# Hybrid trunk layer on one core: the last activation sums spread over four down units, the first down chunk merged, and a later wait in the opening matmuls

## The chip, the cores and the metric

One core of a Trainium2 chip runs the whole layer in float32 precision. The metric is the device time in microseconds (us) of one launch. Engines: TensorE (PE, its weight loads PEld), VectorE (DVE), ScalarE (ACT), GpSimd (POOL) and SyncE (SP), which issues most DMAs; ACT issues the others. `SPq` and `ACTq` in a row are the DMA-issuing instructions of SP and ACT.

## The reference, cut to what matters

```
h  = RMSNorm(x);  p = h @ W_in
y  = concat[SSD(p), sparse attention(p), short conv(p)] @ W_out
x2 = x + y;  h2 = RMSNorm(x2)
g  = causal_conv3(h2 @ W_gate)
out = x2 + (silu(g) * (h2 @ W_up)) @ W_down       # 512 tokens, D = 2048, D_FF = 5632
```

## The kernel before

Every float32 operand is split into a high and a low part in fp32r (`hi = round(x)`, `lo = x - hi`), and a product is three matmuls: hi*hi, lo*hi, hi*lo. ACT makes the high part of a weight block, POOL (for two of seven blocks DVE) the low part.

*The opening.* `quarter` (line 673) multiplies four 128x128 blocks of one projection tile: per block k it issues whi*hhi (L681), wlo*hhi (L682) and whi*hlo (L683). The activations h arrive meanwhile: ACT makes `hhi[k]` (L1137, semaphore `h_hi`), DVE then `hlo[k]` (L1608, `h_lo`). In the first eight quarters those with even n wait for `h_lo` of k ahead of all three matmuls; the odd ones use the same k again. Each quarter first waits for its `wlo` (L599, `lo_ready`).

*The MLP* runs in 44 gate/up units and then 40 down units, called FT, FT+1, ..., FT+39. A unit is one 2x2 block product done with seven products instead of eight (sums of weight blocks times sums of activation blocks). Its positions 0 to 6 each take κ blocks of 128 (κ = 8 in gate/up, 4 or 5 in down). The seven weight operands come from four loaded blocks A21, A22, A11, A12: A21 is copied to PSUM by ACT (`copy_a21`, L1215), DVE forms the sums from it (`sum1`, `sum2`, `sum3_`, `sum4_`), ACT writes `fhi` (`high_unit`, L1208), POOL or DVE `flo` (`low_unit` L629, `low_s1`, `low_s2`), PE multiplies (`product`). All engines run their instructions in the order of the program. While PE is in unit u, ACT does in this order: high 2, high 3, high 4, **copy_a21 of unit u+1**, high 5, high 6, high 0 and high 1 of u+1. POOL does low 3, 4, 5, 6 and low 0 of u+1. SP does, for a unit u, A21 (once `sum3_` of u-1 is done), A22, A11, A12 (once POOL has done low 3 of u-1), and then what hangs behind the unit: `load_x2` and one `load_chunk`.

*Down* goes over five chunks of eight units (one unit per pair of output tiles), κ = 4, 4, 5, 4, 5. Chunk c multiplies by the activation pairs `PAIRS[c]`, brought from HBM by `load_chunk`, seven positions each with a high and a low transfer of 384 KB. The chunk 0 transfers are issued by ACT: positions 0 to 4 in unit FT-1, position 5 behind high 2 and position 6 behind high 3 of unit FT. Those of chunk 1 are issued by SP, one position behind each of the units FT+1 to FT+7. A **merged** unit (`merged(u)`, L869 and L870) joins hi*hi and hi*lo into one matmul 512 wide, since the high and low activations lie side by side; DVE then adds two halves per product (L1840 and L1842) where an unmerged unit (L876 to L878, three matmuls 256 wide) needs one addition (L1842). Before the change all gate/up units and chunks 1 to 4 are merged; chunk 0 (units FT to FT+7) is not, and its fourth block lies in `thi`, `tlo`.

*Where down begins.* The last gate tile is still unfinished in unit FT: ACT's `first_tap` (L1231), two taps on DVE (L1735), ACT's silu (L1291), DVE's `activate` (L1745), and then `act_sums` (L1753, L1754, L1757, L1760), four sums of activation blocks that make the seven operands of the last pair. ACT (L1269, L1270) and POOL (L647, L648) split them in unit FT+1; POOL's last step raises `t_lo` to FP = 22. The residual tiles come back by `load_x2(p)`, for unit FT+p. Four of them (p = 4 to 7) go to places that the activations use until then, so SP waits ahead of them:

```
if u == FT + 3:  sp_.wait_ge(t_lo, FP);  load_x2(4); load_x2(5)
if u == FT + 4:  sp_.wait_ge(f_act, FT); load_x2(6); load_x2(7)
```

Of the kernel before, what the change touches and what calls it, by code (L numbers as in the profile page):

```python
# [169 lines left out]
def hybrid_block(nc, xT, w_in, w_out, w_gu, w_dn, params, relb, cmats, onehot, bias_rows, acs_rows, x2_rows, act_hi, act_lo, out):  # L170
# [4 lines left out]
    with ExitStack() as ctx:  # L175
# [59 lines left out]
        thi = at(RING + 26 * KB, "thi", [P, 7, HT], F32R)  # L235
        tlo = at(RING + 33 * KB, "tlo", [P, 7, HT], F32R)
# [5 lines left out]
        fifth = at(RING + 26 * KB, "fifth", [P, 7, 2, HT], F32R)  # L242
# [213 lines left out]
        def x2_tile(d):  # L456
            return (x2a[:, d, :] if d < 2 else x2b[:, d - 2, :] if d < 6 else x2c[:, d - 6, :] if d < 8 else x2b[:, d - 4, :] if d < 12
                    else x2d[:, d - 12, :] if d < 14 else upv[:, :] if d == 14 else sqsum[:, :])

        def pieces(c, b):  # L460

            half, pairs = 4 * (c % 2), PAIRS[c]
            run = [m for m in pairs[:4] if m < FP - 2]
            found = [(block_of(b)[:, part, half:half + len(run), :], store[b, :, run[0]:run[0] + len(run), :])
                     for part, store in ((HI, act_hi), (LO, act_lo))]
            if len(pairs) == 5:
                found += [(fifth[:, b, part, :], store[b, :, pairs[4], :]) for part, store in ((HI, act_hi), (LO, act_lo))]
            return found
# [126 lines left out]
        def _(pool):  # L595
# [76 lines left out]
        def _(pe):  # L672
            def quarter(slot, n, dst, src_hi, src_lo, ks, first, last, before=None):

                pe.wait_ge(lo_ready, n + 1)
# [182 lines left out]
            def product(u, pos, dst, fresh, before=None):  # L858
# [3 lines left out]
                for k in range(n):  # L862
# [116 lines left out]
        def _(sc):  # L979
# [257 lines left out]
            def unit(n):  # L1237
# [114 lines left out]
        def _(ve):  # L1352
# [495 lines left out]
            def down_unit(n):  # L1848
# [185 lines left out]
```

## Time and profile before

| | us |
|---|---|
| three runs | 2112.37, 2112.72, 2119.51; median 2112.72 |
| the profiled execution | 2116.9 |
| its span, first to last instruction | 2115.1 |
| PE busy in the span | 2104.3 (99%) |
| DVE, POOL, ACT busy | 1555.0, 1276.4, 1008.6 |

The profiled execution is 1.8 us longer than its span. Matmuls are pipelined and their ends are modelled, so progress of PE is read from starts and from its idle times. Engines other than PE have idle time nearly everywhere; the question at each place is whose result PE takes last.

### The profile page before, as it was taken

The numbers are of one execution on the slowest core, as the hardware profiler recorded it, in microseconds if no ns is written. First come the engines' busy times: TensorE is split into PE (matmuls) and PEld (weight loads), VectorE is DVE, ScalarE is ACT, GpSimd is POOL, SyncE is SP. The second block draws the span as 40 slices with busy tenths as digits, with TensorE's granted clock in tenths as the row PEclk, the third lists the DMA queues.
The fourth block names the chain that finished last, engine by engine and source line by source line (L and its number), as shares of the span: only waits on it lengthen the run. The fifth ranks groups of instructions, "written<-read, shape, count | busy, mean of one in ns | idle before, by whom it ended". The sixth has DMA issues, their size and how long they took to land.

```text
span 2115.1 us, 34610 instructions
## 1 busy us (share of the span) xinstructions
PE 2104.3 (99%) x11476; PEld 1782.6 (84%) x11476; DVE 1555.0 (74%) x2756; ACT 1008.6 (48%) x1468; POOL 1276.4 (60%) x731
## 2 busy tenths in 40 slices
PE   9999999999999999999999999999999999999999
PEld 6777777887888888888888888888888899888888
DVE  6489565457663226888888888888888768988987
ACT  6343344434433446545545555555555544444443
POOL 5345334444545656667767767767767676666665
PEclk9999999999999999999999999999999999999999
DMA  6224123233333443344544544544544766655743
GB/s 210 84 74 126 63 69 100 95 105 102 103 99 125 146 145 134 136 164 140 169 154 145 171 144 144 169 152 141 166 151 148 260 222 209 212 187 189 234 130 125
DMA packets 150119, 308.76 MB, mean 146 GB/s; under 512 B 13272, under 2 KB 54424, under 8 KB 149880
## 3 DMA queue, kind: packets, MB, share of 16 engines
q1 hardware_dynamic: 103568, 250.39, 35.3%
q10 hardware_dynamic: 46440, 56.94, 8.6%
q8 instruction: 63, 1.03, 0.2%
q14 instruction: 48, 0.39, 0.1%
HBM read 261.64 MB, written 45.51 MB: 145 GB/s over the span
## 4 chain that ended last, share of the span: by engine, by line
PE 92%; DVE 6%; issue 1%; ACT 0%; DMA 0%; ACTq 0%; SPq 0%; DVEq 0%
PE ps L870 38%; PE ps L869 20%; PE ps L681 10%; PE ps L683 9%; PE ps L682 9%; PE ps L876 1%; PE ps L878 1%; PE ps L877 1%; DVE work L1458 1%; DVE work L1457 1%; DVE work L1361 1%; PE ps L777 1%; DVE work L1360 1%; PE ps L763 0%; PE ps L749 0%
## 5 line engine op out<-in xcount | busy, mean ns | idle before, releaser
L870 PE MATMUL ps<-comb,fhi 128*128 128x512 f32 x3360 | 1180.5, 394 | 0.0
L869 PE MATMUL ps<-comb,flo 128*128 128x256 f32 x3360 | 943.6, 281 | 0.0
L870 PEld LDWEIGHTS ps<-comb,fhi 128*128 128x128 f32 x3360 | 629.8, 187 | 143.9
L629 POOL TENSOR_TENSOR flo<-raw,fhi 128x1024 fp32r<-128x1024 f32 (+2 forms) x252 | 485.0, 1934 | 361.8 <-ACT fhi L1208 361.0
L869 PEld LDWEIGHTS ps<-comb,flo 128*128 128x128 f32 x3360 | 634.4, 189 | 5.6 <-DVE ps L1817 2.2
L599 POOL TENSOR_TENSOR wlo<-raw,whi 128x512 fp32r<-128x512 f32 x260 | 361.4, 1403 | 394.9 <-ACT whi L988 344.1
L629 POOL TENSOR_TENSOR flo<-sum,fhi 128x1024 fp32r<-128x1024 f32 (+2 forms) x168 | 324.0, 1936 | 41.0 <-ACT fhi L1208 40.5
L1208 ACT ACTIVATE fhi<-ps 128x1024 fp32r<-128x1024 f32 (+2 forms) x168 | 141.7, 844 | 420.1 <-DVE ps L1699 242.5
L681 PE MATMUL ps<-hhi,whi 128*128 128x512 f32 x784 | 317.3, 405 | 2.4 <-DVE hlo L1608 2.4
L683 PE MATMUL ps<-hlo,whi 128*128 128x512 f32 x784 | 306.4, 391 | 0.0
L682 PE MATMUL ps<-hhi,wlo 128*128 128x512 f32 x784 | 305.7, 390 | 0.0
L1208 ACT ACTIVATE fhi<-raw 128x1024 fp32r<-128x1024 f32 (+2 forms) x252 | 219.4, 871 | 45.7 <-PE ps L870 36.2
L681 PEld LDWEIGHTS ps<-hhi,whi 128*128 128x128 f32 x784 | 147.2, 188 | 49.3 <-issue 13.9
L683 PEld LDWEIGHTS ps<-hlo,whi 128*128 128x128 f32 x784 | 147.1, 188 | 31.8
L682 PEld LDWEIGHTS ps<-hhi,wlo 128*128 128x128 f32 x784 | 147.4, 188 | 30.5 <-issue 2.2
L1208 ACT ACTIVATE fhi<-sum 128x1024 fp32r<-128x1024 f32 (+2 forms) x168 | 146.1, 870 | 16.1 <-PE ps L870 11.2
L988 ACT ACTIVATE whi<-raw 128x512 fp32r<-128x512 f32 x200 | 118.5, 621 | 61.0 <-PE ps L683 33.0
L682 PE MATMUL ps<-yhi,wlo 128*128 128x512 f32 x256 | 99.6, 389 | 0.0
L683 PE MATMUL ps<-ylo,whi 128*128 128x512 f32 x256 | 99.6, 389 | 0.0
L681 PE MATMUL ps<-yhi,whi 128*128 128x512 f32 x256 | 99.6, 389 | 0.0
L1215 ACT ACTIVATE ps<-raw 128x1024 f32<-128x1024 f32 (+2 forms) x84 | 70.6, 841 | 35.7 <-DVE sum L1716 32.0
L1675 DVE TENSOR_TENSOR ps<-ps,raw 128x1024 f32<-128x1024 f32 (+2 forms) x84 | 83.5, 995 | 4.9 <-DMA raw<-w_gu 4.0
(246 smaller groups left out, 2799.2 us busy)
## 6 DMA issues: line engine op xcount, KB each, us to landing
raw<-w_gu SPq DMA_DIRECT2D x176, 512.0 KB, 3.4
raw<-w_in SPq DMA_DIRECT2D x196, 256.0 KB, 3.2
raw<-w_dn SPq DMA_DIRECT2D x96, 256.0 KB, 2.9
raw<-w_dn SPq DMA_DIRECT2D x64, 320.0 KB, 3.1
act_hi<-thi ACTq DMA_DIRECT2D x20, 896.0 KB, 4.2
act_lo<-tlo ACTq DMA_DIRECT2D x20, 896.0 KB, 8.2
raw<-w_out SPq DMA_DIRECT2D x64, 256.0 KB, 3.2
comb<-act_hi SPq DMA_DIRECT2D x21, 512.0 KB, 3.9
```

Of the source, the lines that this page charges most:

```text
L599: nc.gpsimd.tensor_tensor(wlo[:, slot % NW, 0:width], raw[:, slot % NRAW, 0:width], whi[:, slot % NW, 0:width].bitcast(F32), ALU.subtract) ...
L629: nc.gpsimd.tensor_tensor(flo[s][:, 0:w], src[:, 0:w], fhi[s][:, 0:w].bitcast(F32), ALU.subtract).then_inc(f_lo_pool, 1)
L681: nc.tensor.matmul(dst, whi[:, s, w], src_hi[:, k, :], start=first and i == 0, stop=False)
L682: nc.tensor.matmul(dst, wlo[:, s, w], src_hi[:, k, :], start=False, stop=False)
L683: ins = nc.tensor.matmul(dst, whi[:, s, w], src_lo[:, k, :], start=False, stop=last and i == len(ks) - 1)
L777: nc.tensor.matmul(ps[:, 2 + hh, 0:P * (b + 1)], qkT[rows, h // 2, b * P:(b + 1) * P], qkT[rows, 4 + h // 2, 0:P * (b + 1)], start=True, s ...
L869: nc.tensor.matmul(dst[:, 0:HT], flo[s][:, w], both[:, HI, :], start=fresh and k == 0, stop=False, skip_group_check=True)
L870: ins = nc.tensor.matmul(dst, fhi[s][:, w], both, start=False, stop=k == n - 1, skip_group_check=True)
L988: A(whi[:, slot % NW, 0:width], raw[:, slot % NRAW, 0:width], ACT.Copy).then_inc(hi_ready, 1)
L1208: A(fhi[s][:, 0:w], src[:, 0:w], ACT.Copy).then_inc(f_hi, 1)
L1215: A(wide(LEFT)[:, 0:width(u)], raw21[:, 0:width(u)], ACT.Copy).then_inc(copied21, 1)
L1675: V.tensor_tensor(wide(RIGHT)[:, 0:w], wide(LEFT)[:, 0:w], raw22[lane(u) % 2][:, 0:w], ALU.add).then_inc(sum1_ready, 1)
```

## The change

1. Opening: a quarter with even n waits for `h_hi` ahead of the first two matmuls of a block and for `h_lo` only ahead of the third.
2. Unit FT keeps three matmuls; FT+1 to FT+7 become merged. `thi` and `tlo` become the halves of one tile `pair_sums`, which is also what chunks 2 and 4 used as `fifth`.
3. ACT in unit FT: the transfers of position 5 are issued behind `first_tap`, those of position 6 behind high 4.
4. The four last sums on DVE leave unit FT: one in each of FT+1 and FT+2, two in FT+3. ACT's and POOL's split of them moves from unit FT+1 to FT+4.
5. SP: behind unit FT+3 it waits for `f_act` and loads x2 for p = 4 and 5 (now to `x2d`, `upv`, `sqsum`); behind unit FT+5 it waits for `t_lo` = FP and loads p = 6 and 7 (now to `x2b`).

```diff
         def merged(u):
-            return gate_up(u) or u >= FT + NPAIR
+            return gate_up(u) or u > FT
+        def apart(u, k):
+            return not gate_up(u) and k == (3 if u < FT + NPAIR else 4)
...
-                if u == FT + 3:
-                    sp_.wait_ge(t_lo, FP)
+                if u == FT + 3:
+                    sp_.wait_ge(f_act, FT)
                     load_x2(4)
                     load_x2(5)
-                if u == FT + 4:
-                    sp_.wait_ge(f_act, FT)
+                if u == FT + 5:
+                    sp_.wait_ge(t_lo, FP)
                     load_x2(6)
                     load_x2(7)
...
# POOL, behind low 0 of the next unit (ACT the same, behind high 4)
-                if lane(n) % 2 == 1 and n != 1 and (gate_up(n) or n == FT + 1):
+                if lane(n) % 2 == 1 and n != 1 and gate_up(n) or n == FT + 4:
...
# quarter()
                     nc.tensor.matmul(dst, wlo[:, s, w], src_hi[:, k, :], start=False, stop=False)
+                    if between is not None:
+                        between(k)
                     ins = nc.tensor.matmul(dst, whi[:, s, w], src_lo[:, k, :], start=False,
...
-                        (lambda k: pe.wait_ge(h_lo, k + 1)) if n % 2 == 0 else None)
+                        (lambda k: pe.wait_ge(h_hi, k + 1)) if n % 2 == 0 else None,
+                        (lambda k: pe.wait_ge(h_lo, k + 1)) if n % 2 == 0 else None)
...
# ACT, unit FT
-                if n == FT:
-                    load_chunk(sc, 0, 5)
                 sc.wait_ge(loaded12, lin(n, 16, 16))
                 high_unit(n, 3, raw12)
-                if n == FT:
-                    load_chunk(sc, 0, 6)
...
                     first_tap(step(n, -1))
+                if n == FT:
+                    load_chunk(sc, 0, 5)
                 sc.wait_ge(sum3_ready, lin(n, 1, 1))
                 high_unit(n, 4, sum3)
+                if n == FT:
+                    load_chunk(sc, 0, 6)
...
# DVE, down_unit
+            def last_sum(i):
+                buf = act[(FP - 1) % 2]
+                to, a, b = ((2, 0, 1), (4, 6, 0), (3, 6, 2), (5, 7, 3))[i]
+                ve.wait_ge(f_act, FT)
+                ve.wait_ge(t_sum, 4 * (FP - 1) + (0, 0, 1, 3)[i])
+                V.tensor_tensor(buf[:, to, :], buf[:, a, :], buf[:, b, :], ALU.subtract).then_inc(t_sum, 1)
...
+                if 1 <= v <= 3:
+                    last_sum(v - 1)
                 accumulate(v, 3, 0, early, xbank(n))
...
-                if tail:
-                    act_sums(n, 2)
+                if v == 3:
+                    last_sum(3)
```

## Rows read from the trace of the kernel before

**Rows 1.** The page: busy times of the engines; shares of the chain that ended last.
```profile
PE 2104.3 (99%) x11476; PEld 1782.6 (84%) x11476; DVE 1555.0 (74%) x2756; ACT 1008.6 (48%) x1468; POOL 1276.4 (60%) x731
...
PE 92%; DVE 6%; issue 1%; ACT 0%; DMA 0%; ACTq 0%; SPq 0%; DVEq 0%
```

**Rows 2.** Waits of PE, whole span: total us, times, longest.
```profile
PE ps L681 <- DVE hlo L1608: 2.4, 2, 1.6
...
PE ps L876 <- DVE x2a L1842: 1.5, 1, 1.5
```

**Rows 3.** Timeline of the opening: start, us, engine, line, operation, [idle before].
```profile
5.80 1.27 POOL L599 TENSOR_TENSOR wlo<-raw,whi 128x512 fp32r<-128x512 f32 x1 [5.34 <-ACT whi L988]
...
7.76 0.47 PE L681 MATMUL ps<-hhi,whi 128*128 128x512 f32 x1 [1.64 <-DVE hlo L1608]
...
9.31 1.41 DVE L1608 SCALAR_TENSOR_TENSOR hlo<-resid,pc,hhi 128x512 fp32r<-128x512 f32 x2 [1.03 <-ACT hhi L1137]
...
10.12 0.50 PE L681 MATMUL ps<-hhi,whi 128*128 128x512 f32 x1 [0.73 <-DVE hlo L1608]
...
10.69 0.40 PE L683 MATMUL ps<-hlo,whi 128*128 128x512 f32 x1
```

**Rows 4.** PE timeline: first matmuls of units FT+1, FT+4, FT+8, FT+15.
```profile
1685.86 0.28 PE L876 MATMUL ps<-comb,fhi 128*128 128x256 f32 x1
...
1716.22 0.28 PE L876 MATMUL ps<-comb,fhi 128*128 128x256 f32 x1
...
1756.54 0.28 PE L869 MATMUL ps<-comb,flo 128*128 128x256 f32 x1
...
1825.35 0.28 PE L869 MATMUL ps<-comb,flo 128*128 128x256 f32 x1
```

**Rows 5.** Timelines of ACT, DVE and PEld in unit FT.
```profile
1674.11 2.28 ACTq L480 DMA_DIRECT2D comb<-act_hi  x1
1676.41 0.46 ACTq L480 DMA_DIRECT2D comb<-act_lo  x1
1676.99 0.69 ACT L1231 ACTIVATE ps<-gpad,pc 128x512 f32<-128x512 f32 x1 [2.33 <-issue]
...
1682.39 1.49 DVE L1754 TENSOR_TENSOR act<-act 128x256 f32<-128x256 f32 x1
...
1684.32 0.19 PEld L876 LDWEIGHTS ps<-comb,fhi 128*128 128x128 f32 x1 [1.65 <-DMA comb<-act_lo]
```

**Rows 6.** DMA issues between 1676.41 and 1676.7: KB, us to landing.
```profile
comb<-act_lo ACTq DMA_DIRECT2D x1, 384.0 KB, 7.5
```

**Rows 7.** The page, DMA issues of the whole span: one group.
```profile
raw<-w_dn SPq DMA_DIRECT2D x96, 256.0 KB, 2.9
```

**Rows 8.** DVE timeline: one act_sums, and DVE's idle in merged unit FT+10.
```profile
1685.99 0.41 DVE L1760 TENSOR_TENSOR act<-act 128x256 f32<-128x256 f32 x1
...
1780.64 0.42 DVE L1840 TENSOR_TENSOR x2b<-ps,x2b 128x256 f32<-128x256 f32 x1 [0.49 <-PE ps L870]
```

**Rows 9.** POOL timeline, end of unit FT+1.
```profile
1698.22 0.74 POOL L648 TENSOR_TENSOR comb<-act,comb 128x256 fp32r<-128x256 f32 x1
```

**Rows 10.** SP timeline, behind A12 of unit FT+3, then behind A12 of FT+5.
```profile
1700.63 0.94 SPq L531 DMA_DIRECT2D x2b<-x_rows  x2
1701.68 0.40 SPq L480 DMA_DIRECT2D comb<-act_hi  x1
...
1703.19 6.08 SPq L522 DMA_DIRECT2D raw<-w_dn  x4
...
1719.46 0.37 SPq L480 DMA_DIRECT2D comb<-act_hi  x1
...
1723.34 6.09 SPq L522 DMA_DIRECT2D raw<-w_dn  x4
```

**Rows 11.** ACT and POOL: copy of A21 to low 5, in unit FT+3.
```profile
1709.80 0.60 ACT L1215 ACTIVATE ps<-raw 128x512 f32<-128x512 f32 x1 [1.33 <-DMA raw<-w_dn]
...
1711.03 1.29 POOL L629 TENSOR_TENSOR flo<-sum,fhi 128x512 fp32r<-128x512 f32 x1 [1.13 <-ACT fhi L1208]
```

More of the change, by code:

```diff
@@ L234, in hybrid_block @@
         act = [at(RING + 10 * KB + 8 * KB * i, f"act{i}", [P, 8, HT]) for i in range(2)]
-        thi = at(RING + 26 * KB, "thi", [P, 7, HT], F32R)
-        tlo = at(RING + 33 * KB, "tlo", [P, 7, HT], F32R)
+        pair_sums = at(RING + 26 * KB, "pair_sums", [P, 7, 2, HT], F32R)
+        thi, tlo = pair_sums[:, :, 0, :], pair_sums[:, :, 1, :]
         x2b = at(RING + 10 * KB, "x2b", [P, 8, T])
@@ L239, in hybrid_block @@
         x2d = at(yq(6, 1), "x2d", [P, 2, T])
-        fifth = at(RING + 26 * KB, "fifth", [P, 7, 2, HT], F32R)
         ctx.enter_context(nc.sbuf_tensor("reserved", [P, (EXTRA + 16 * KB) // 4], F32))
@@ L456, in x2_tile @@
         def x2_tile(d):
-            return (x2a[:, d, :] if d < 2 else x2b[:, d - 2, :] if d < 6 else x2c[:, d - 6, :] if d < 8 else x2b[:, d - 4, :] if d < 12
-                    else x2d[:, d - 12, :] if d < 14 else upv[:, :] if d == 14 else sqsum[:, :])
+            return (x2a[:, d, :] if d < 2 else x2b[:, d - 2, :] if d < 6 else x2c[:, d - 6, :] if d < 8 else x2d[:, d - 8, :] if d < 10
+                    else upv[:, :] if d == 10 else sqsum[:, :] if d == 11 else x2b[:, d - 8, :])
         def pieces(c, b):
@@ L466, in pieces @@
             if len(pairs) == 5:
-                found += [(fifth[:, b, part, :], store[b, :, pairs[4], :]) for part, store in ((HI, act_hi), (LO, act_lo))]
+                found += [(pair_sums[:, b, part, :], store[b, :, pairs[4], :]) for part, store in ((HI, act_hi), (LO, act_lo))]
             return found
@@ L524, in load_x2 @@
             def load_x2(p):
-                if p == NPAIR - 1:
+                if p == 5:
                     sp_.dma_start(upv[:, :], x2_rows[2 * p]).then_inc(x2_loaded[p], 16)
@@ L529, in load_x2 @@
                     return
-                dst = {1: x2b[:, 0:2, :], 2: x2b[:, 2:4, :], 3: x2c[:, :, :], 4: x2b[:, 4:6, :], 5: x2b[:, 6:8, :], 6: x2d[:, :, :]}[p]
+                dst = {1: x2b[:, 0:2, :], 2: x2b[:, 2:4, :], 3: x2c[:, :, :], 4: x2d[:, :, :], 6: x2b[:, 4:6, :], 7: x2b[:, 6:8, :]}[p]
                 sp_.dma_start(dst, x2_rows[2 * p:2 * p + 2].rearrange("d p t -> p d t")).then_inc(x2_loaded[p], 16)
@@ L639, in unit @@
                     low_unit(step(n, 1), 0, raw11)
-                if lane(n) % 2 == 1 and n != 1 and (gate_up(n) or n == FT + 1):
-                    m = lin(n, 1, -3) // 2 if isinstance(n, int) else 2 * n[0] + (n[1] - 3) // 2
+                if lane(n) % 2 == 1 and n != 1 and gate_up(n) or n == FT + 4:
+                    m = FP - 1 if n == FT + 4 else (n - 3) // 2 if isinstance(n, int) else 2 * n[0] + (n[1] - 3) // 2
                     pool.wait_ge(t_hi, m + 1)
-                    if n == FT + 1:
+                    if n == FT + 4:
                         last = act[(FP - 1) % 2]
@@ L672, in _, with quarter @@
         def _(pe):
-            def quarter(slot, n, dst, src_hi, src_lo, ks, first, last, before=None):
+            def quarter(slot, n, dst, src_hi, src_lo, ks, first, last, before=None, between=None):
                 pe.wait_ge(lo_ready, n + 1)
@@ L866, in product @@
                     if merged(u):
-                        both = fifth[:, b] if k == 4 and not gate_up(u) else block_of(b)[:, :, half + k, :]
+                        both = pair_sums[:, b] if apart(u, k) else block_of(b)[:, :, half + k, :]
                         nc.tensor.matmul(dst[:, 0:HT], flo[s][:, w], both[:, HI, :], start=fresh and k == 0, stop=False, skip_group_check=True)
@@ L871, in product @@
                         continue
-                    if u < FT + NPAIR and k == 3:
+                    if apart(u, k):
                         high, low = thi[:, b, :], tlo[:, b, :]
@@ L1262, in unit @@
                     load_chunk(sc, 0, 0)
-                if lane(n) % 2 == 1 and n != 1 and (gate_up(n) or n == FT + 1):
-                    m = pair_of(n)
+                if n == FT:
+                    load_chunk(sc, 0, 6)
+                if lane(n) % 2 == 1 and n != 1 and gate_up(n) or n == FT + 4:
+                    m = FP - 1 if n == FT + 4 else pair_of(n)
                     sc.wait_ge(t_sum, 4 * m + 4)
-                    if n == FT + 1:
+                    if n == FT + 4:
                         last = act[(FP - 1) % 2]
@@ L1858, in down_unit @@
                 if v < NPAIR:
-                    ve.wait_ge(x2_loaded[v], 16 if v < NPAIR - 1 else 32)
+                    ve.wait_ge(x2_loaded[v], 32 if v == 5 else 16)
                 accumulate(v, 1, 0, late, xbank(n))
@@ L1877, in down_unit @@
                     sum3_(n + 1)
-                if tail:
-                    act_sums(n, 0)
                 ve.wait_ge(d_add, 7 * v + 2)
```

3 lines of the change are left out of this document (removed).

## The prediction

> **What bounds the kernel now.** I read the page first: PE is busy 2104.3 of 2115.1 us, and the chain that ended last is PE for 92% and DVE for 6% [rows 1]. So whatever is gained must be idle time of PE or spacing between its matmuls, and whatever makes another engine late counts only when PE has to wait for it. The list of PE's waits comes next: of its few entries two lie at the places of this change, 2.4 us in two waits for `hlo` (the opening) and one of 1.5 us for DVE in unit FT [rows 2]. Last come the timelines at both places, for what arrives last there, and SP's timeline around the moved loads.
>
> PE's pace: from FT+4 to FT+8 four unmerged units take 1756.54 - 1716.22 = 40.32 us, 10.08 each, with no gap; from FT+8 to FT+15 seven merged ones take 68.81 us, 9.83 each [rows 4].
>
> **Step 1, the opening.** The first real matmul starts at 7.76, released by hlo[0]; but `wlo` of the quarter, for which PE waits in any case, is ready only at 5.80 + 1.27 = 7.07 [rows 3]. The high parts come earlier. So the first block starts near 7.2, and its third matmul, which still needs hlo[0], near 7.73 instead of two matmuls after 7.76: about 0.55 earlier. That lead dies at block 2, where PE waits again: hlo[2] releases it at 10.12, and the third matmul is at 10.69 [rows 3]. DVE started hlo[2] at 9.31, as soon as ACT had hhi[2], so the two high matmuls can run between 9.4 and 10.0 and the third goes at about 10.12 to 10.15. The gain that remains is 10.69 - 10.13 = 0.55 us. After that block PE waits for `hlo` no more (two waits in all [rows 2]), and everything there is made from the loads and not from PE's progress. Later, around 90 to 200 us, DVE is on the chain; it is fed by PE's results there, so I let the lead pass, with 0 as the other bound. **-0.55.**
>
> **Step 2, unit FT.** The wait named for PE is DVE's, which did two of the sums ahead of an addition that PE's position 6 wanted; the second of them alone holds DVE from 1682.39 for 1.49 us. The sums go, and `first_tap` no longer stands behind a transfer whose issue held ACT for 2.28 us: `first_tap` ran at 1676.99 after 2.33 us of idle ACT [rows 5]. With both gone the addition ends some 2 us earlier, about 1682.2, in time for PE, which was ready at 1684.32 - 1.65 = 1682.67. But the weight load that PE resumed with, at 1684.32, is put down to something else, the transfer of `act_lo` [rows 5], issued at 1676.41 and landed 7.5 us later, at 1683.9 [rows 6]. That is the new last arrival. And the change issues it later: position 5 behind `first_tap` (1675.3 and 1675.7), position 6 behind high 4, which waits for DVE's `sum3` (1676.7) and takes 0.6, so at about 1677.4 and 1677.8, 1.4 later than before. At 7.5 us it would land at 1685.3, and PE would resume 1.1 us later than now. A 256 KB piece lands in 2.9 us in the median of the span [rows 7]; at that pace, 1680.7, it would cost nothing, a gain of 1.65 and with a short wait for low 4 ahead of it 2.1. The transfers of position 5 are out of the way later too, and the same bytes have to pass, so I take the middle: PE resumes where it does now. **0, between -2.1 and +1.1.** If the 2.28 us hold of ACT comes again it stands ahead of high 4 instead of `first_tap`, and then costs up to the same 1.1.
>
> The Trainium skill ("DMA: Bandwidth & Descriptors", section "Queues, rings and completion order") says that each DMA engine takes turns between the queues that have work for it. Here SP puts 512 KB pieces into its queue from 1677 on, so by that rule ACT's late pieces would get half the engines; a landing of 7.5 us for 384 KB agrees with a shared stretch. By that rule step 2 would be nearer its upper end, +1.1.
>
> **Step 3, merged units.** 10.08 - 9.83 = 0.25 us less per unit [rows 4]. Not the third matmul's cost: the columns are the same, 768 per block, only the start intervals are shorter. Five units get it freely (FT+1 to FT+3, FT+6, FT+7), FT+4 and FT+5 are counted in step 5. DVE pays 7 more additions per unit, and had 0.49 idle in the one gap of a merged unit [rows 8]; so it is close to being the bound but not it, as seven units of chunk 1 show. 5 x 0.25: **-1.2.** Bounds: 0 (DVE eats it) and -1.4.
>
> **Step 4, the last sums.** Each is 0.41 us of DVE, some 0.35 when pipelined [rows 8]. In FT+1 and FT+2 one fits into the 0.49. FT+3 has two: 0.7 to 0.8 against 0.49. **+0.2**, between 0 and +0.9.
>
> **Step 5, SP waits for the split of the last sums.** This is the term that decides. SP issues in order. Behind A12 of FT+5 it will wait for `t_lo` = FP and only then issue load_x2(6), load_x2(7), one `load_chunk`, and after these **A21, A22, A11 and A12 of unit FT+6**. Take S4 = start of unit FT+4 on PE, S5 and S6 the next ones.
> - When SP is there: A12(FT+5) is issued once POOL has done low 3 of FT+4; what is behind it stands at 1719.46 with S4 = 1716.22, S4 + 3.2. The next A21 is at 1723.34, S4 + 7.1 [rows 4, 10].
> - When `t_lo` comes: the split has moved from POOL's unit FT+1 to its unit FT+4, behind low 0 of the next unit. In FT+1 it ended at 1698.22 + 0.74 = 1698.96 with that unit's start at 1685.86: start + 13.1 [rows 4, 9]. So S4 + 13.1, and SP sits for 9.9 us. Before, the waiting unit was two units behind the splitting one (FT+3 and FT+1): SP passed at 1700.63, 1.7 after `t_lo`, and the wait cost nothing [rows 9, 10].
> - A21(FT+6) is then issued at about S4 + 15.0 (two x2 issues, two of the chunk, 0.4 to 0.5 each). It was copied by ACT at S5 + 2.4 = S4 + 12.2 in the ordinary run of things (the copy of FT+4's A21, which waited 1.33, ran at 1709.80, so ACT was ready for it at 1708.5, in unit FT+3, which started 10.08 ahead of 1716.22, at 1706.14) [rows 4, 11]. So it is late however fast it lands.
> - When it lands: the same sequence (two x2 pieces, one chunk position, A21) stood behind FT+3. From the first issue at 1700.63 to the copy that waited for A21, 1709.80, are 9.2 us [rows 10, 11]. In the new place the queue is empty before it, so 8.8: S4 + 13.2 + 8.8 = S4 + 22.0.
> - What is queued behind: ACT stands at copy_a21(FT+6) and with it high 5 and 6 of FT+5 and high 0 and 1 of FT+6; DVE stands at sum1(FT+6). Copy to low 5 on POOL is 1711.03 - 1709.80 = 1.23, low 5 takes 1.29, and 0.1 to PE [rows 11]: PE's position 5 of FT+5 starts at S4 + 24.65. It would want S4 + 9.83 + 5 x 1.40 = 16.85. Two positions later, S6 = S4 + 27.45. Low 6 and low 0 follow POOL's low 5 at 1.29 each, in time; DVE catches up in the same stretch.
> - Also in it: POOL's low 3 of FT+5 comes behind the split, at S4 + 14.4, where PE wants it at 14.0; 0.4 us that vanish in the larger stall.
>
> Before, S6 - S4 was 20.16. **+7.3.** Bounds: A21 landing in 2.9 us [rows 7] gives S6 = S4 + 17.9 + 2.65 + 2.8 = 23.35, so +3.2; the full 9.2 and a ragged restart, +8.
>
> **Sum**, against the profiled execution: -0.55 + 0 - 1.2 + 0.2 + 7.3 = +5.75, so 2116.9 + 5.75 = 2122.7 (span 2115.1 + 5.75, and 1.8 around it). That execution was 4.2 above the median of the runs, 2112.72, and the difference is not in the trace's parts that change; on the median it is **2118.5 us**. The other steps (other places for x2 tiles, `pair_sums` for `fifth`) move the same bytes at the same rate: nothing.
>
> **Rivals.**
> - *The hold of SP costs nothing* (it ends faster). It would need A21(FT+6) landed by S4 + 12.2, so `t_lo` by S4 + 3.4; below that point each us is a us of PE. For it speaks only that the trace before had the same wait for free, against it the program order on POOL. Price: FT+4 and FT+5 merged, 2 x 0.25 less and 0.4 for low 3, so -1.65 in all, and -3.7 if unit FT loses its stall too: 2109.0 to 2111.1, say 2110.5. 12%.
> - *The hold costs, but the queue empties fast.* A21 lands between S4 + 17.9 [rows 7] and S4 + 20, halfway to the forecast's 22.0: total +1.6 to +3.7, 2114.3 to 2116.4. For it: nothing else is in flight in that hold. Against: 9.2 us in rows 10 and 11, with little else in flight either. 23%.
> - *The transfers of positions 5 and 6 come too late as well*, and DVE falls behind in FT+3: +1.1 and +0.9 on top, 2119.5 to 2122. 13%.
> - That the opening doesn't gain, since `wlo` comes last, is inside the forecast: 7.07 bounds it.
>
> The Trainium skill ("DMA: Bandwidth & Descriptors", section "Anatomy of one DMA") prices a transfer at 2.0 us fixed and its bytes at 436 GB/s (a fit for another issue path). An estimate by it for the 2.0 MB up to and with A21: 6.8 us instead of 8.8, the landing at S4 + 20.0, 2116.5; the 2.9 us of a quiet 256 KB piece agrees with it (2.6), the 9.2 of the full sequence does not.
>
> **How the numbers follow.** Forecast 52%, rivals 12, 23 and 13%. The forecast's own range is 2116.5 to 2120.5. The range of 8 in 10 reaches over the fast-queue case and most of the last: 2113.0 to 2122.5, also since one of three runs before was 6.8 above the others. What a measurement can tell from no change is some 0.5%, 10.6 us: faster than 2102.2 is in no case (1%), slower than 2123.3 needs the worst ends together (4%), within it 95%. The sign is slower with 0.86.
>
> **What would show it.** In the changed trace: PE's first matmul near 7.2 and the first wait for `hlo` at a third matmul; in unit FT PE resumes position 6 released by DMA, not by DVE; merged units FT+1 and FT+2 take 9.8; SP idle for some 10 us behind A12 of FT+5, released by POOL, and in unit FT+5 one PE idle time of about 7.8 us ahead of position 5, with ACT waiting for `raw<-w_dn` at L1215. If there is no PE gap above 1 us in FT+5 or FT+6, the forecast is wrong and the kernel should be faster; if the gap is 3 to 5 us, only the landing was mis-sized.

## The result: the changed kernel is slower by 0.2 to 0.4%

| | before | after |
|---|---|---|
| median of 9 runs each | 2112.72 | 2121.63 (2119.87 to 2125.9), ratio 1.0039 [1.0027, 1.0051] |
| a second comparison, 35 and 12 runs | 2113.67 | 2118.65 (2115.24 to 2125.26), ratio 1.0021 [1.0007, 1.0035] |
| profiled execution / its span | 2116.9 / 2115.1 | 2121.12 / 2119.2 |

The forecast, 2118.5, is a ratio of 1.0027. By the prediction's bound of 0.5% this is no change in either comparison, but both intervals exclude 1. The medians differ by 8.9 and by 5.0 us, for a forecast of 5.8, and two terms were off; both have to be explained. The three comparisons below ran on three chips (medians of the kernel before: 2111.18, 2113.67 and 2117.06), so a median is set beside its own comparison only.

Lines have moved by 3 to 6 in the changed kernel: L681 and L683 are L684 and L688; L869 and L870 are L875 and L876; L876 to L878 are L882 to L884; `high_unit` is L1214, `copy_a21` L1221, `low_unit` L632.

The page after, busy times (for [rows 1]):
```profile
PE 2103.6 (99%) x11280; PEld 1776.3 (84%) x11280; DVE 1570.8 (74%) x2805; ACT 1008.4 (48%) x1468; POOL 1275.6 (60%) x731
...
PE 91%; DVE 6%; DMA 1%; issue 1%; ACT 1%; POOL 0%; SPq 0%; ACTq 0%; DVEq 0%
```
PE has 196 matmuls less (7 units x 28 blocks, merged), DVE 49 additions more (7 x 7), and DMA has come into the chain. The waits of PE after, total, times, longest (for [rows 2]):
```profile
PE ps L875 <- POOL flo L632: 6.2, 1, 6.2
PE ps L837 <- DVE work L1596: 1.5, 1, 1.5
PE ps L809 <- DVE work L1552: 0.9, 1, 0.9
PE ps L684 <- POOL wlo L602: 0.9, 1, 0.9
PE ps L684 <- ACT hhi L1143: 0.7, 1, 0.7
PE ps L882 <- DMA comb<-act_lo: 0.6, 1, 0.6
```
The waits for `hlo` and for DVE in unit FT are gone from this list. Three short ones stand in their places (`wlo`, `hhi`, `act_lo`), and there is one new wait, by far the longest: 6.2 us for low 5. It is in unit FT+5. Starts on PE of units FT, FT+4, FT+6 and FT+8 after (for [rows 4]):
```profile
1673.35 0.28 PE L882 MATMUL ps<-comb,fhi 128*128 128x256 f32 x1
...
1713.81 0.28 PE L875 MATMUL ps<-comb,flo 128*128 128x256 f32 x1
...
1742.59 0.28 PE L875 MATMUL ps<-comb,flo 128*128 128x256 f32 x1
...
1762.29 0.28 PE L875 MATMUL ps<-comb,flo 128*128 128x256 f32 x1
```
FT to FT+8 is 88.94 us, against 82.93 before (1673.61 to 1756.54). So the profiled pair's +4.1 of span is -0.26 up to unit FT, +6.01 in these eight units, and -1.6 in the remaining 357 us, which the change leaves as they were but for the places of tiles (that last figure is no effect of the change; see the last section).

The timeline after, around the hold: SP's issues, then who was released by them.
```profile
1711.42 6.27 SPq L525 DMA_DIRECT2D raw<-w_dn  x4
1726.89 0.89 SPq L534 DMA_DIRECT2D x2b<-x_rows  x2
1727.89 0.40 SPq L483 DMA_DIRECT2D comb<-act_hi  x1
1728.33 0.43 SPq L483 DMA_DIRECT2D comb<-act_lo  x1
1728.86 2.37 SPq L525 DMA_DIRECT2D raw<-w_dn  x4
...
1734.86 0.60 ACT L1221 ACTIVATE ps<-raw 128x512 f32<-128x512 f32 x1 [8.63 <-DMA raw<-w_dn]
1735.56 0.70 DVE L1681 TENSOR_TENSOR ps<-ps,raw 128x512 f32<-128x512 f32 x1 [6.30 <-DMA raw<-w_dn]
1736.08 1.27 POOL L632 TENSOR_TENSOR flo<-sum,fhi 128x512 fp32r<-128x512 f32 x1 [6.72 <-ACT fhi L1214]
...
1737.41 0.58 PE L875 MATMUL ps<-comb,flo 128*128 128x256 f32 x1 [6.16 <-POOL flo L632]
...
1738.22 0.42 PE L875 MATMUL ps<-comb,flo 128*128 128x256 f32 x1
...
1738.86 0.42 PE L875 MATMUL ps<-comb,flo 128*128 128x256 f32 x1
```
Read it downwards. SP has issued the weights of FT+5 and then issues nothing for 9.2 us (1711.42 + 6.27 = 1717.69 to 1726.89): it stands at the wait for `t_lo`. Then it first issues two x2 tiles and two chunk transfers, and only at 1728.86 the A21 of unit FT+6. ACT, DVE and POOL have been idle for 6 to 9 us when it lands, and all of them and PE resume within 2.6 us. So what looks like a stall of every engine at once, with the DMA engines full, is here one late load. The last two rows show something more: blocks follow at 1738.86 - 1738.22 = 0.64 us, where a merged block otherwise takes 0.35.

Stretches of 5 us after (us, busy of PE, PEld, DVE, ACT, POOL, granted clock, DMA share, GB/s):
```profile
1730.00:1735.00 5.00, 1.25 (x7) 0.80 (x5) 0.00 (x0) 0.14 (x1) 0.00 (x0) 1.00 1.04 391
1735.00:1740.00 5.00, 2.59 (x8) 2.31 (x9) 3.40 (x7) 2.52 (x5) 3.75 (x3) 0.56 0.84 300
1740.00:1745.00 5.00, 5.00 (x23) 4.29 (x23) 3.59 (x8) 1.86 (x3) 1.30 (x1) 0.76 0.30 96
```
After 6.16 us of idle time PE is granted 0.56 and then 0.76 of its clock, so for part of both stretches the lower of its two levels, 1.2 instead of 2.4 GHz. Positions 5 and 6 take 2.73 and 2.45 us instead of 1.4 each.

### The profile page after: what moved, and what is told of

Read it like the earlier page. It is cut to its first block, busy times and chain, and to the rows that moved or that the text cites. A ratio compares the mean times of both kernels' runs of the same rounds, so it can differ in the third digit from the quotient of the medians.

```text
span 2119.2 us, 34271 instructions
## 1 busy us (share of the span) xinstructions
PE 2103.6 (99%) x11280; PEld 1776.3 (84%) x11280; DVE 1570.8 (74%) x2805; ACT 1008.4 (48%) x1468; POOL 1275.6 (60%) x731
## 4 chain that ended last, share of the span: by engine, by line
PE 91%; DVE 6%; DMA 1%; issue 1%; ACT 1%; POOL 0%; SPq 0%; ACTq 0%; DVEq 0%
PE ps L876 40%; PE ps L875 20%; PE ps L684 10%; PE ps L688 9%; PE ps L685 9%; DVE work L1464 1%; DVE work L1463 1%; DVE work L1367 1%; DVE work L1366 1%; PE ps L782 1%; PE ps L768 0%; PE ps L754 0%; DVE work L1455 0%; DVE work L1442 0%; PE ps L823 0%
## 5 line engine op out<-in xcount | busy, mean ns | idle before, releaser
L876 PE MATMUL ps<-comb,fhi 128*128 128x512 f32 x3507 | 1234.5, 395 | 0.0
L875 PE MATMUL ps<-comb,flo 128*128 128x256 f32 x3507 | 987.7, 282 | 6.2 <-POOL flo L632 6.2
L876 PEld LDWEIGHTS ps<-comb,fhi 128*128 128x128 f32 x3507 | 659.6, 188 | 146.7
L632 POOL TENSOR_TENSOR flo<-raw,fhi 128x1024 fp32r<-128x1024 f32 (+2 forms) x252 | 484.7, 1934 | 360.9 <-ACT fhi L1214 360.5
L875 PEld LDWEIGHTS ps<-comb,flo 128*128 128x128 f32 x3507 | 664.1, 189 | 12.8 <-POOL flo L632 6.6
L632 POOL TENSOR_TENSOR flo<-sum,fhi 128x1024 fp32r<-128x1024 f32 (+2 forms) x168 | 323.9, 1934 | 46.8 <-ACT fhi L1214 46.6
L1214 ACT ACTIVATE fhi<-ps 128x1024 fp32r<-128x1024 f32 (+2 forms) x168 | 141.7, 843 | 421.4 <-DVE ps L1705 255.9
L684 PE MATMUL ps<-hhi,whi 128*128 128x512 f32 x784 | 317.7, 405 | 1.5 <-POOL wlo L602 0.9
L688 PE MATMUL ps<-hlo,whi 128*128 128x512 f32 x784 | 307.0, 392 | 0.1
L1214 ACT ACTIVATE fhi<-raw 128x1024 fp32r<-128x1024 f32 (+2 forms) x252 | 219.4, 871 | 41.2 <-PE ps L876 39.2
L684 PEld LDWEIGHTS ps<-hhi,whi 128*128 128x128 f32 x784 | 147.4, 188 | 47.8 <-issue 13.9
L688 PEld LDWEIGHTS ps<-hlo,whi 128*128 128x128 f32 x784 | 147.2, 188 | 32.8 <-DVE hlo L1614 0.9
L1214 ACT ACTIVATE fhi<-sum 128x1024 fp32r<-128x1024 f32 (+2 forms) x168 | 146.1, 870 | 14.2 <-PE ps L876 12.4
L684 PE MATMUL ps<-yhi,whi 128*128 128x512 f32 x256 | 99.7, 390 | 0.0
L688 PE MATMUL ps<-ylo,whi 128*128 128x512 f32 x256 | 99.7, 389 | 0.0
L1221 ACT ACTIVATE ps<-raw 128x1024 f32<-128x1024 f32 (+2 forms) x84 | 70.6, 841 | 47.1 <-DVE sum L1722 34.0
L1681 DVE TENSOR_TENSOR ps<-ps,raw 128x1024 f32<-128x1024 f32 (+2 forms) x84 | 83.5, 994 | 10.3 <-DMA raw<-w_dn 6.3
```

What stands on the lines that cost most here:

```text
L632: nc.gpsimd.tensor_tensor(flo[s][:, 0:w], src[:, 0:w], fhi[s][:, 0:w].bitcast(F32), ALU.subtract).then_inc(f_lo_pool, 1)
L684: nc.tensor.matmul(dst, whi[:, s, w], src_hi[:, k, :], start=first and i == 0, stop=False)
L875: nc.tensor.matmul(dst[:, 0:HT], flo[s][:, w], both[:, HI, :], start=fresh and k == 0, stop=False, skip_group_check=True)
L876: ins = nc.tensor.matmul(dst, fhi[s][:, w], both, start=False, stop=k == n - 1, skip_group_check=True)
L1214: A(fhi[s][:, 0:w], src[:, 0:w], ACT.Copy).then_inc(f_hi, 1)
L1221: A(wide(LEFT)[:, 0:width(u)], raw21[:, 0:width(u)], ACT.Copy).then_inc(copied21, 1)
```

## The experiments

All stand on the changed kernel unless it is said. "Stretch" is FT to FT+8 by PE's starts in the profiled execution: 82.93 before, 88.94 after.

**1. `sp_later`: the wait and what it guards one unit later.**
```diff
-                if u == FT + 5:
+                if u == FT + 6:
                     sp_.wait_ge(t_lo, FP)
                     load_x2(6)
                     load_x2(7)
```


> The changed kernel with one edit: the wait for t_lo = FP and load_x2(6), load_x2(7) stand behind unit FT+6 on SP instead of FT+5. Theory (the hold of SP in FT+5 is the whole loss): PE's idle of 6.2 us ahead of position 5 of FT+5 and the stretch at the lower clock behind it go; from the start of FT+4 to that of FT+6 take 20.0 to 20.2 us instead of 28.8 (two merged units of 9.83 and 0.4 for POOL's low 3, which still comes behind the split). The kernel then ends some 3 us below the one before the change: 2109 to 2111, ratio 0.998 to 0.9995. Rival (the merged units or the later transfers cost, the hold only hides it): a new PE wait of over 1 us appears in FT+3 to FT+7 and the time stays above 2113.

Measured: 2109.49 (2107.61 to 2113.4, 11 runs) beside 2111.18 (33 runs), ratio 0.9991 [0.9982, 1.0000]; stretch 80.35. FT+4 starts at 1716.88, POOL's split ends at 1729.99, and SP is at the wait only after that (timeline of `sp_later`, POOL and SP):
```profile
1729.24 0.75 POOL L651 TENSOR_TENSOR comb<-act,comb 128x256 fp32r<-128x256 f32 x1
```
```profile
1725.13 6.47 SPq L525 DMA_DIRECT2D raw<-w_dn  x3
1731.65 0.94 SPq L534 DMA_DIRECT2D x2b<-x_rows  x2
```
```profile
1736.98 0.28 PE L875 MATMUL ps<-comb,flo 128*128 128x256 f32 x1
```
The wait costs nothing where it now stands, 1.66 us behind the split, as the same wait did before the change. FT+4 and FT+5 take 1736.98 - 1716.88 = 20.10 us instead of 28.78. The whole loss was in the place of one wait and of the two loads behind it; experiment 3 parts them. The 20.10 lies in the expected range for a reason only partly right: of the 0.44 us above two units of 9.83, some 0.3 is not low 3 but a late addition of DVE, told under steps 3 and 4.

**2. `warm`: PE kept busy in the gap** by 24 extra matmuls into an unused bank, ahead of position 5 of FT+5 (they add no result).
```diff
+                    if v == 5 and pos == 5:
+                        for _ in range(24):
+                            nc.tensor.matmul(bank(X), comb[:, 0, HI, 0, 0:P], block_of(0)[:, :, 0, :], ...)
```


> The changed kernel with 24 matmuls more, 512 wide, on PE ahead of its wait for position 5 of unit FT+5; they read activations that lie in SBUF and write a PSUM bank that nobody uses at that time, 24 x 0.23 = 5.5 us of the 6.2 us idle. Theory (the lower clock behind the idle costs by itself): the granted clock stays 1.00 from 1735 to 1745, positions 5 and 6 of FT+5 take 1.4 us each instead of 2.73 and 2.45, the unit is 2.2 to 2.5 us shorter (16.3 instead of 18.64), and the time is 2 to 2.5 us under that of the changed kernel. Rival (the slow positions are the refill of ACT, POOL and DVE behind the hold): the unit stays 18.5 or so whatever the clock.

Measured: 2116.21 (2114.42 to 2125.71, 11 runs) beside the same 2111.18, ratio 1.0024 [1.0015, 1.0034]. PE in `warm`, and its stretches (columns as above):
```profile
1736.24 5.65 PE L942 MATMUL ps<-comb 128*128 128x512 f32 x24
1742.71 0.39 PE L875 MATMUL ps<-comb,flo 128*128 128x256 f32 x1 [0.82 <-POOL flo L632]
```
```profile
1735.00:1740.00 5.00, 5.00 (x25) 4.13 (x25) 0.00 (x0) 0.00 (x0) 0.00 (x0) 1.00 1.04 403
1740.00:1745.00 5.00, 4.18 (x22) 3.25 (x21) 3.86 (x9) 2.67 (x5) 3.62 (x3) 1.00 0.80 297
```
The load is as late as before (DMA at 403 GB/s, three engines idle), but the clock stays at 1.00, and from position 5 to S6 it takes 2.93 us instead of 5.18 (after) and 4.40 (after, second trace). So the lowered clock costs 1.5 to 2.3 us here, and the wait itself the rest. This is read from the traces; the ratio of `warm` lies between the two ratios of the changed kernel (1.0039 and 1.0021), so the runs alone don't show it. The Trainium skill ("TensorE: Matmul & The Clock Gate", section "What's actually happening") has the rule: "the default state is throttled, and activity releases the throttle". The traces agree with it (0.56 behind the gap, 1.00 with the gap filled), and with it the forecast could have had this term.

**3. `hold_only`: the wait stays behind FT+5, the two x2 loads go behind FT+6.**
```diff
                 if u == FT + 5:
                     sp_.wait_ge(t_lo, FP)
+                if u == FT + 6:
                     load_x2(6)
                     load_x2(7)
```


> The changed kernel with load_x2(6) and load_x2(7) behind unit FT+6, but the wait for t_lo = FP kept behind FT+5. It tells the hold from the 1 MB in the queue ahead of A21(FT+6). Theory (both count, the hold first): A21 is issued 0.9 us earlier and has 0.77 MB less... 1.0 MB less ahead of it; ACT copies it at start of FT+4 + 18 to 19 instead of + 21.05, PE idles 3 to 4 us instead of 6.2, and the time is 2.5 to 4 us under that of the changed kernel. If the hold alone mattered (landing 3 us behind an issue): + 17, idle 2 us. If the bytes alone mattered: no idle of PE above 1 us.

Measured: 2114.82 (2112.37 to 2116.19, 10 runs), ratio 1.0014 [1.0004, 1.0023]; stretch 88.02. ACT and PE in `hold_only`:
```profile
1730.21 0.60 ACT L1222 ACTIVATE ps<-raw 128x512 f32<-128x512 f32 x1 [6.79 <-DMA raw<-w_dn]
```
```profile
1732.76 0.58 PE L876 MATMUL ps<-comb,flo 128*128 128x256 f32 x1 [4.40 <-POOL flo L633]
```
FT+4 starts at 1710.96, so A21 lands by S4 + 19.25 (after: 21.05). 1 MB of x2 ahead of it costs 1.8 us; the wait alone still leaves PE idle for 4.4 us, and the clock is lowered all the same (0.70 and 0.62 in the two stretches from 1730), so that S6 - S4 is 27.1. The wait for `t_lo` alone makes 7.0 of the 8.7 us between `sp_later` and the changed kernel, the loads in front of A21 the rest. The landing and the idle time are a little above what was expected (18 to 19 and 3 to 4); the expectation had no term for the clock. The loads without the wait were not tried.

**4. `opening_only`: the kernel before, with step 1 alone.**
```diff
+                        (lambda k: pe.wait_ge(h_hi, k + 1)) if n % 2 == 0 else None,
                         (lambda k: pe.wait_ge(h_lo, k + 1)) if n % 2 == 0 else None)   # ahead of the third matmul
```


> The kernel before with the opening part of the change alone. Theory: PE's third matmul of block 2 starts near 10.15 instead of 10.69, 0.54 us earlier, and the lead is kept to the end: time 0.5 us under that of before, which a measurement can't tell from none (ratio 0.998 to 1.002). Rival: the lead is lost again where DVE is on the chain, 90 to 200 us, so that PE's start behind it differs by under 0.2 us.

Measured: 2110.73 (2108.95 to 2113.72, 10 runs) beside 2111.18, ratio 1.0000 [0.9990, 1.0009]. In its profile PE is 0.44 us ahead up to 155 us and 0.29 from 203 us on, where PE waits for DVE's `work` (L1391) 0.5 us against 0.4 before; gate/up starts at 811.00 against 811.29. Some 0.15 of the lead is given back at that wait. 0.29 us is below what the runs can tell.

**5. `after_again`: the changed kernel, unaltered,** in one comparison with the next three.

> The changed kernel once more, unaltered, to be compared on the chip and in the rounds of the next three. Its trace showed 5.0 to 5.5 us more than the kernel before in the stretches that the change touches, its runs 8.9 us. Theory (the rest is the spread of runs): the ratio comes out nearer 1.0025 than 1.004, and the stretch from the start of unit FT to that of FT+8 takes 88.9 us again. Rival (something outside the stretch costs 3 to 4 us in every run): ratio 1.004 or more again.

Measured: the second row of the first table; stretch 88.23, FT 11.12, FT+4 and FT+5 28.0. The stretch is the same to 0.7 us; most of the 3 us between the two medians of the changed kernel is not in it.

**6. `unmerged`: `sp_later` with FT+1 to FT+7 in three matmuls again.**
```diff
-            return gate_up(u) or u > FT
+            return gate_up(u) or u >= FT + NPAIR
```


> The kernel sp_later with chunk 0 unmerged as before the change. Theory (a merged unit saves 0.25 us): FT+1 to FT+7 take 10.08 each but for FT+5 with about 10.2, the stretch from FT to FT+8 takes 1.7 us more than in sp_later (80.35), 82.0; time +1.7 us, below what 3 rounds tell apart. Rival (DVE's seven further additions eat the saving): the stretch is within 0.5 us of sp_later's.

Measured: 2115.15 (10 runs) beside 2113.67, ratio 0.9994 [0.9980, 1.0009]; units 10.08 us each again (FT+5 10.19), stretch 81.76 against 80.35. Merging is worth 1.4 us over seven units, 0.20 each, where [rows 4] gave 0.25.

**7. `old_order`: `sp_later` with ACT's transfers of positions 5 and 6 at their places before the change** (behind high 2 and high 3, ahead of `first_tap`). The last sums stay spread.
```diff
                     high_unit(n, 2, wide(LEFT))
+                if n == FT:
+                    load_chunk(sc, 0, 5)
                 sc.wait_ge(loaded12, lin(n, 16, 16))
                 high_unit(n, 3, raw12)
...
+                if n == FT:
+                    load_chunk(sc, 0, 6)
...
                     first_tap(step(n, -1))
-                if n == FT:
-                    load_chunk(sc, 0, 5)
                 sc.wait_ge(sum3_ready, lin(n, 1, 1))
                 high_unit(n, 4, sum3)
...
-                if n == FT:
-                    load_chunk(sc, 0, 6)
```


> The kernel sp_later with the transfers of positions 5 and 6 issued by ACT where they were before the change, behind high 2 and high 3 of unit FT. It tells what shortened FT from 12.25 to 10.96 us. Theory (first_tap ahead of the transfers does it, since the additions and low 4 follow from it): FT is 11.8 to 12.3 us long, with a wait of 0.4 or more ahead of position 4 and one ahead of position 6, released by DMA, of 1.3 to 1.6. Rival (the sums' leaving DVE does it): FT stays at 11.0 to 11.2, with no wait ahead of position 4.

Measured: 2113.0 (12 runs), ratio 0.9989 [0.9974, 1.0004]; stretch 81.92, FT 12.60 (before 12.25, after 10.96). ACT in `old_order`, then the weight load of position 6:
```profile
1671.64 2.49 ACTq L483 DMA_DIRECT2D comb<-act_lo  x1
1674.26 0.69 ACT L1237 ACTIVATE ps<-gpad,pc 128x512 f32<-128x512 f32 x1 [2.43 <-issue]
```
```profile
1681.84 0.19 PEld L882 LDWEIGHTS ps<-comb,fhi 128*128 128x128 f32 x1 [1.82 <-DMA comb<-act_lo]
```
Without the sums DVE is not late, and unit FT is as long as it was: position 4 waits 0.35 us for low 4, and the weights of position 6 wait 1.82 us for the transfer. One trace each would not be enough here, since unit FT differs from one execution to the next, but the twelve traces together bear it out, with one overlap. With ACT's old order it took 12.25, 11.82 and 12.90 us with the sums in it (`before`, `before_again`, `opening_only`) and 12.60 without; with the new order it took 10.96 to 11.64 in seven kernels or traces, and 12.19 in `x2_later`. So ACT's order, not the sums, shortened unit FT, by about 1.1 us.

**8. `x2_later`: `sp_later` with `load_x2(2)` and `load_x2(3)` behind FT+2 instead of FT+1,** to take SP's bytes out of the way of ACT's last transfer.
```diff
-                if u == FT + 1:
+                if u == FT + 2:
                     load_x2(2)
                     sp_.wait_ge(up_part, 2 * FT)
                     load_x2(3)
```


> The kernel sp_later with load_x2(2) and load_x2(3), 1 MB, behind unit FT+2 instead of FT+1 on SP. In unit FT PE waits 0.8 to 1.3 us ahead of position 6 for the last act_lo transfer of position 6, which lands 6.7 us behind its issue. Theory (SP's transfers share the DMA engines with it): it lands within 4.5 to 5.5 us, the wait is under 0.3 us, FT takes 10.1 to 10.4 us instead of 11.1, and the time is 0.8 us under that of sp_later. Rival (the order in ACT's own queue sets the landing): FT stays at 11.0 or more.

Measured: 2113.36 (12 runs), ratio 0.9989 [0.9979, 0.9999]; FT 12.19, not the 10.1 to 10.4 expected. It was no cleaner: the two chunk 1 transfers behind them moved up in their place, and an issue held ACT for 1.84 us, so that the last `act_lo` was issued at S(FT) + 3.21 and landed 7.4 us later. Inconclusive, hence the next.

**9. `quiet_sp`: `sp_later` with nothing but weights and the first x2 piece from SP until behind FT+2.**
```diff
-                if u == FT + 1:
+                if u == FT + 2:
                     load_x2(2)
+                    load_chunk(sp_, 1, 0)
+                if u == FT + 3:
                     sp_.wait_ge(up_part, 2 * FT)
                     load_x2(3)
...
                     load_x2(4)
+                if u == FT + 4:
                     load_x2(5)
```


> The kernel sp_later with nothing of SP's in the DMA queues, but weights and the first x2 piece, while ACT's transfers of positions 5 and 6 land: load_x2(2) and position 0 of chunk 1 stand behind unit FT+2, load_x2(3) and (4) behind FT+3, load_x2(5) behind FT+4. In x2_later the 1 MB of x2 alone was moved and its place in the queue was taken at once by chunk 1's 768 KB. Theory (it is the share of the engines, whoever takes it): the last act_lo lands 4.5 to 5.5 us behind its issue instead of 6.7 to 7.4, the wait ahead of position 6 is under 0.3 us, FT takes 10.1 to 10.5 us; time 0.7 us under sp_later's, which is below what the rounds tell apart. Rival (ACT's four pieces set their own landing): FT stays at 11.0 or more.

Measured: 2115.26 (12 runs) beside 2117.06 (17), ratio 0.9992 [0.9978, 1.0005]; stretch 80.60, FT 11.05. The last `act_lo` lands 6.5 us after its issue (after: 6.7), and position 6 still waits:
```profile
1686.78 0.19 PEld L882 LDWEIGHTS ps<-comb,fhi 128*128 128x128 f32 x1 [0.93 <-DMA comb<-act_lo]
```
The bulk that SP issues behind FT+1 is not what makes it late; what is left is ACT's own 384 KB pieces, the weights and the first x2 piece. Which of these sets the 6.5 us stays open.

**10. `before_again`: the kernel before, one more profiled execution,** for the scatter of its trace.

> The kernel before, unaltered, for a second trace: how much its stretches differ from one execution to the next. Theory: the stretch from the start of FT to that of FT+8 is 82.9 to 83.7 us again and gate/up starts at 811.3; what differs beyond 1 us lies in the pace of the matmuls, 0.347 or 0.353 us per merged pair, over long stretches. Rival: the stretch itself moves by over 1 us.

Measured: 2112.4, span 2110.6; stretch 82.51, FT 11.82, position 6 waiting 1.5 us again. ACT's last issue ahead of `first_tap`, its landing, and the weight load of position 6:
```profile
1674.29 0.86 ACTq L480 DMA_DIRECT2D comb<-act_lo  x1
```
```profile
comb<-act_lo ACTq DMA_DIRECT2D x1, 384.0 KB, 9.5
```
```profile
1683.78 0.19 PEld L876 LDWEIGHTS ps<-comb,fhi 128*128 128x128 f32 x1 [1.71 <-DMA comb<-act_lo]
```
The stretch is 0.4 us shorter than expected. `opening_only`, whose code is the same there, took 83.69, so the stretch itself moves by 1.2 us, nearly all of it in unit FT.

## Why the prediction was right, and where it was off

The sign, the step that decides and the size (forecast 2118.5; medians 2121.63 and 2118.65) came out. The first of the two is 3.1 us above the forecast, and the stretches that the change touches don't hold that difference. Point by point, by the first profiled pair:

**Step 1: right at its place, halved later.** PE's first and second wait in the opening after, and the third matmul of block 2 (for [rows 3]):
```profile
6.95 0.50 PE L684 MATMUL ps<-hhi,whi 128*128 128x512 f32 x1 [0.87 <-POOL wlo L602]
...
9.36 0.51 PE L684 MATMUL ps<-hhi,whi 128*128 128x512 f32 x1 [0.67 <-ACT hhi L1143]
...
10.15 0.50 PE L688 MATMUL ps<-hlo,whi 128*128 128x512 f32 x1
```
10.69 became 10.15, -0.54 for -0.55. The other bound, "DVE takes it back", holds for part: -0.26 is left at unit FT.

**Step 2: 0 forecast, -1.29 measured** (12.25 to 10.96; about -1.1 over all traces). The releaser was named rightly (DMA instead of DVE), and the time of the last issue was wrong. The prediction said that high 4 "waits for DVE's `sum3` (1676.7)". The addition that ended there was another one, `sum4_`; the `sum3` of this unit was long done. ACT and its DMA issues in unit FT after (for [rows 5]), the last transfer's landing (issue, size, median us to landing; for [rows 6]), and the weight load:
```profile
1673.80 0.33 ACTq L483 DMA_DIRECT2D comb<-act_hi  x1
1674.14 0.68 ACT L1237 ACTIVATE ps<-gpad,pc 128x512 f32<-128x512 f32 x1
1674.16 1.30 ACTq L483 DMA_DIRECT2D comb<-act_lo  x1
1675.57 0.63 ACT L1214 ACTIVATE fhi<-sum 128x512 fp32r<-128x512 f32 x1 [0.74 <-PE ps L884]
...
1676.01 0.51 ACTq L483 DMA_DIRECT2D comb<-act_lo  x1
```
```profile
comb<-act_lo ACTq DMA_DIRECT2D x1, 384.0 KB, 6.7
```
```profile
1682.78 0.19 PEld L882 LDWEIGHTS ps<-comb,fhi 128*128 128x128 f32 x1 [0.85 <-DMA comb<-act_lo]
```
An issue did not wait here for the activation ahead of it: the first one, behind `first_tap` in the program, starts at 1673.80 and `first_tap` at 1674.14. But an activation behind a held issue did: high 4 ran at 1675.57, straight behind the 1.30 us issue. So the last transfer was issued at S(FT) + 2.66 and not + 4.2 (S(FT) is the start of the unit); before it was + 2.80 (1676.41 - 1673.61). It wasn't later at all, it landed 0.8 sooner after its issue, and position 6 resumes 1.28 us earlier measured from the unit's start. Since `first_tap` no longer stands behind the hold, the chain on DVE follows in time. `old_order` shows that this order is the gain.

The prediction also erred in how it reckoned the landing, as an issue time and so many us. In `before_again` the last transfer was issued at S(FT) + 0.80, 2.0 us sooner than in `before`, took 9.5 us instead of 7.5, and landed at + 10.3 like the other; after the change it lands at + 9.4. So its issue did not set its landing. That SP's pieces would take ACT's share and bring this step near +1.1 did not come true either, and with most of them away (`quiet_sp`) the last piece landed only 0.2 us sooner after its issue. Why the new order brings the landing forward by about 1 us is open.

**Steps 3 and 4: -1.0 forecast together, -0.86 measured** in FT+1 to FT+3 and -0.46 in FT+6 and FT+7. The merged units take 9.81, 9.83, 9.86; two sums in FT+3 cost 0.03 to 0.05 us of PE in that unit and not 0.2. `unmerged` confirms the size of merging. But the second sum of FT+3 is paid one unit later. In the kernel after, DVE's fourth sum, its addition for position 1 of FT+4, and the weight load of position 2, which waits for that addition:
```profile
1714.09 0.41 DVE L1774 TENSOR_TENSOR act<-act 128x256 f32<-128x256 f32 x1
...
1716.26 0.42 DVE L1856 TENSOR_TENSOR x2d<-ps,x2d 128x256 f32<-128x256 f32 x1
...
1716.80 0.19 PEld L875 LDWEIGHTS ps<-comb,flo 128*128 128x128 f32 x1 [0.37 <-issue]
```
DVE has no idle time between the two, so the sum makes that addition late. FT+4 takes 10.14 to 10.16 us in every kernel with merged units here, and 10.08, an unmerged unit's usual time, in `unmerged`, where DVE has fewer additions. The 0.3 us is hidden by the hold in the changed kernel and paid in `sp_later`. No run moved this sum alone, so this is read from rows.

**Step 5: +7.3 forecast, +8.62 measured, two errors of opposite sign.** With S4 = 1713.81: `t_lo` at S4 + 13.05 (forecast 13.1), A21 issued at + 15.05 (15.0), copied by ACT, as soon as it had landed, at + 21.05 (22.0), PE's position 5 at + 23.60 (24.65), S6 at + 28.78 (27.45). So the term of the landing, 7 us from A21's issue, was 1.0 too large: the 2.0 MB passed in 1734.86 - 1726.89 = 7.97 us. The Trainium skill's estimate in the prediction ("DMA: Bandwidth & Descriptors", section "Anatomy of one DMA"), 6.8 us, was 1.2 too short; the truth lay between the page and [rows 10, 11]. And the missing term was the clock: positions 5 and 6 took 5.18 instead of 2.80, +2.4, of which `warm` gives back 2.25.

**Sum over the eight units and the opening:** forecast +5.75, measured -0.26 + 6.01 = +5.75. That they are equal to the hundredth is luck: step 2 was forecast 1.3 too high and step 5 1.3 too low, step 1 gained 0.3 less than forecast and merging 0.3 more.

**The rivals.** That the hold costs nothing: refuted, 6.2 us of PE idle. That the queue empties fast (landing at S4 + 17.9 to 20): missed by 1 us. That the late transfers cost more: refuted in unit FT, which became shorter; that DVE falls behind in FT+3 showed as 0.3 us in FT+4, not 0.9.

**Best version.** `sp_later` keeps the change's gains (-0.3 in the opening, -1.1 in unit FT, -1.4 by merging) and none of its loss but the 0.3 us in FT+4: stretch 80.35 against 82.93, ratio 0.9991 [0.9982, 1.0000]. That is as much as 0.1% and at the edge of what 11 runs can tell from nothing.

## What to carry to other kernels

A wait on an engine that issues DMAs in order holds everything behind it: list what is queued behind it in its new place, and compare the time at which the engine arrives there with the time at which the semaphore is raised, once more whenever either end is moved. Here one unit of lookahead made the difference between 9.2 us of hold and none. Where a change makes PE idle for several microseconds, add the slower clock after the gap to the price of the gap; and where a term of a sum hangs on which semaphore an instruction waits for, read it in the code and not from the nearest row in time. In unit FT a landing time was not an issue time plus a constant: issued 2.0 us sooner, the last transfer landed at the same time.

## What the runs showed of the hardware that was not expected

**The clock after a gap.** 6.2 us and 4.4 us without matmuls (`after`, `hold_only`) were each followed by a lowered granted clock (0.56 and 0.76; 0.70 and 0.62); with the gap filled it stayed at 1.00. The shorter gap did not cost less: positions 5 and 6 took 5.18 and 4.40 us behind 6.2 and 6.1 us of idle time (the two traces of the changed kernel), 5.29 behind 4.4 us in `hold_only`, and 2.93 in `warm`.

**An issue that holds ACT.** In every trace one DMA issue of ACT near unit FT takes 0.9 to 3.1 us, where most of them take 0.3 to 0.5: 2.28, 0.86 and 3.12 in `before`, `before_again` and `opening_only`, 2.49 in `old_order`, and 1.29 to 1.84 in the eight with ACT's new order. It is one of the row of 384 KB pieces of positions 5 and 6, but not always the same one (position 5's in the kernel after, position 6's in `old_order`). The cause is open.

**Two paces at full clock.** The unchanged rest of the kernel differs by more than the change is worth. Groups of the kernel before in two stretches of 90 us, both at a granted clock of 1.00 and without a wait (count, busy, mean ns, idle):
```profile
L870 PE MATMUL ps<-comb,fhi 128*128 128x512 f32 x260 | 90.3, 391 | 0.0
```
```profile
L870 PE MATMUL ps<-comb,fhi 128*128 128x512 f32 x256 | 90.5, 399 | 0.0
```
The first is 1270 to 1360, the second 1390 to 1480. By starts, a merged block follows the last at 0.347 or at 0.353 us in the mean, in long stretches of one or the other. Summed over a trace, what lies above 0.3467 per block is some 10.8 us before and 6.2 in `before_again`; without it their times are 2106.1 and 2106.2. In the same way: after 2111.2, `after_again` 2109.8, `hold_only` 2110.8, `warm` 2108.9, `sp_later` 2102.4, `unmerged` 2103.4, `opening_only` 2107.0. This pace, whose cause is open, differs by as much as single runs do, and between the two profiles of the changed kernel it makes up 1.7 of 3.2 us (9.9 against 8.2 in excess). By the times without it the change costs 3.6 to 5.1 us and `sp_later` gains 3.7. That it also makes the scatter of the runs without a profile is a guess.
